# Scores of two neighbourhood heads issued in turn to the two row halves, and scores two heads ahead of the transposes

## The reference

```python
h = rmsnorm_2(x, norm_mix[i])
proj = h @ w_in[i]
na_q, na_k, na_v, q_lat, kv_lat, k_rope, gate_a, gate_b = jnp.split(proj, IN_CUTS, axis=-1)
y_a = neighbourhood_attention(na_q.reshape(B, S, 8, 64), na_k..., na_v..., na_rpb[i]) @ w_na_o[i]
y_b = latent_attention(q_lat, kv_lat, k_rope, ...) @ w_mla_o[i]      # 8 heads, 64 + 32 dims for scores, 64 for values
merged = jax.nn.sigmoid(gate_a) * y_a + jax.nn.sigmoid(gate_b) * y_b
x = x + merged @ w_out[i]
x = x + expert_choice_moe(...)                                       # 16 experts, 384 MB of weights in the two layers
x = x + ple_gate * (p[i] @ ple_w[i])
```

## Time and profile before

| | us |
|---|---|
| median of 3 runs | 1995.76 (1995.65 to 1997.39) |
| the profiled execution | 1993.96 |
| its span in the profile | 1991.8 |
| PE busy | 1591.3 (80%) |
| DVE, ACT, POOL busy | 609.5, 503.2, 188.5 |

### The profile page before, as it was taken

The page is one execution under the profiler, slowest core; times in us unless marked ns, Lnnn a source line. Parts: engine busy times, 40 slices in busy tenths (PEclk is TensorE's granted clock), DMA queues, the critical chain, the costliest instruction groups (busy, mean ns, idle before and its releaser), DMA issues.

```text
span 1991.8 us, 29539 instructions
## 1 busy us (share of the span) xinstructions
PE 1591.3 (80%) x12524; PEld 1158.8 (58%) x12524; DVE 609.5 (31%) x915; ACT 503.2 (25%) x914; POOL 188.5 (9%) x214
## 2 busy tenths in 40 slices
PE   7999999999998998576665666998997566666566
PEld 6999899998897875232222224996774232222225
DVE  3557433676644342000000003554350000000005
ACT  3534233456443432000000003443330000000003
POOL 0042000110321100000000002310100000000002
PEclk9999999999999999887888988998998888888888
DMA  8464748333554319999999997643259999999994
GB/s 286 155 216 156 262 154 264 95 101 114 181 152 151 106 67 425 428 424 423 428 425 425 427 427 291 207 144 135 75 204 427 424 424 427 425 425 427 425 426 140
DMA packets 167949, 563.64 MB, mean 283 GB/s; under 512 B 10591, under 2 KB 122107, under 8 KB 134952
## 3 DMA queue, kind: packets, MB, share of 16 engines
q1 hardware_dynamic: 159952, 552.05, 71.3%
q10 hardware_dynamic: 7896, 10.13, 1.5%
HBM read 561.08 MB, written 5.23 MB: 284 GB/s over the span
## 4 chain that ended last, share of the span: by engine, by line
PE 50%; DMA 38%; DVE 4%; issue 3%; ACT 2%; POOL 1%; ACTq 0%; DVEq 0%; SPq 0%; POOLq 0%
DMA ring<-in_moe_w 36%; PE bank L920 25%; PE bank L1152 6%; PE bank L879 4%; PE bank L1517 3%; PE bank L1210 2%; DMA big<-in_moe_w 2%; PE bank L1050 2%; PE bank L1538 1%; PE bank L1219 1%; PE bank L1082 1%; PE bank L992 1%; DVE ring_r L1985 1%; ACT big L1643 1%; PE bank L1405 1%
## 5 line engine op out<-in xcount | busy, mean ns | idle before, releaser
L1517 PE MATMUL bank<-ring,big 128*32 128x256 f32 x3840 | 284.3, 446 | 198.8 <-DMA ring<-in_moe_w 197.5
L920 PE MATMUL bank<-big_r,ring_r 128*128 128x256 f32 x2736 | 347.8, 288 | 0.0
L1517 PEld LDWEIGHTS bank<-ring,big 128*32 128x32 f32 x3840 | 148.7, 124 | 339.7 <-issue 300.5
L920 PEld LDWEIGHTS bank<-big_r,ring_r 128*128 128x128 f32 x2736 | 339.5, 196 | 1.6 <-issue 0.9
L1985 DVE TENSOR_TENSOR ring_r<-ring,ring_r 128x2048 fp32r<-128x2048 f32 (+2 forms) x105 | 243.3, 2322 | 150.8 <-ACT ring_r L1596 149.6
L1643 ACT ACTIVATE big<-bank 128x512 f32<-128x512 f32 (+2 forms) x186 | 88.0, 490 | 574.5 <-PE bank L879 353.5
L1538 PE MATMUL bank<-ring,big 128*32 128x512 f32 x1024 | 143.9, 653 | 83.0 <-DMA ring<-in_moe_w 65.9
L1596 ACT ACTIVATE ring_r<-ring 128x2048 fp32r<-128x2048 f32 (+2 forms) x109 | 204.2, 1881 | 13.0 <-issue 5.4
L879 PE MATMUL bank<-big 128*128 128x128 f32 (+2 forms) x630 | 106.6, 297 | 66.5 <-ACT big L1643 24.1
L2368 DVE SCALAR_TENSOR_TENSOR big<-big,bank 128x256 f32<-128x256 f32 x32 | 13.5, 421 | 476.4 <-ACT big L1887 476.4
L1152 PE MATMUL bank<-ring_r,big_r 128*128 128x512 f32 x576 | 137.0, 397 | 2.5 <-DVE big_r L1992 2.1
(11 more groups left out here) (198 smaller groups left out, 1422.9 us busy)
## 6 DMA issues: line engine op xcount, KB each, us to landing
ring<-in_moe_w SPq DMA_DIRECT2D x120, 2048.0 KB, 23.7
ring<-in_moe_w SPq DMA_DIRECT2D x128, 1024.0 KB, 25.1
ring<-in_w_in SPq DMA_DIRECT2D x28, 1024.0 KB, 5.4
ring<-in_od_w_in SPq DMA_DIRECT2D x22, 1024.0 KB, 6.7
ring<-in_ev_w_in SPq DMA_DIRECT2D x20, 1024.0 KB, 6.4
big<-in_moe_w SPq DMA_DIRECT2D x8, 2048.0 KB, 20.0
ring<-in_ev_w_out SPq DMA_DIRECT2D x8, 1024.0 KB, 4.9
ring<-in_od_cmp_w SPq DMA_DIRECT2D x8, 1024.0 KB, 8.6
```

Of the source, the lines that this page charges most:

```text
L920: ins = unit[0].mark(mm(dst, lhsT, rhs, start=start and n == 0, stop=stop and n == len(terms) - 1))
L1517: ins = mm(banks[5 + up][32 * j:32 * j + 32, 0:256], xg[:, k, q, :], wv[:, r, 256 * j:256 * (j + 1)], start=k == 0, stop=k == KC - 1)
```

## The change

`paired` now issues the scores of heads 0 and 1 ahead of the first fill, and the scores of head h + 2 directly behind the transposes of head h. This moves the same steps on all four engines. `pT` moves ahead of V14, V15. On PE a new function, `pair_scores`, issues the scores of two neighbourhood heads together: their matmuls alternate between the lower and the upper 64 rows, and go to banks 3 and 4. It stands at the even head's place; at the odd head's PE does nothing. Its wait is that DVE has taken the maximum of the pair before (and so has read both banks). The latent heads keep `scores`. The order on PE becomes:

```diff
@@ paired
-    out = [("S", 0)] + take()
+    out = [("S", 0), ("S", 1)] + take()
     for h in range(heads):
-        if h + 1 < heads:
-            out += [("S", h + 1)]
-        out += [("T", h)] + take()
+        out += [("T", h)] + ([("S", h + 2)] if h + 2 < heads else []) + take()
         if h % 2:
             out += [("V", h - 1), ("V", h)]
@@ LAYER
-         + [(e[0], e[1] + NAH) if e[0] != "proj" else e for e in _ML]
-         + [("pT", 0)] + proj("yb", 0, 1, 2, 3) + [("out", 2)])
+         + [(e[0], e[1] + NAH) if e[0] != "proj" else e for e in _ML[:-2]]
+         + [("pT", 0)] + [(e[0], e[1] + NAH) for e in _ML[-2:]] + proj("yb", 0, 1, 2, 3) + [("out", 2)])
@@ tensor engine
+            def pair_scores(l, h, i):
+
+                if h == 0:
+                    pe.wait_ge(exp_done, 2 * i)
+                    for nm in ("nak", "nav"):
+                        for c in range(2):
+                            wait_evicted(pe, l, nm, c)
+                else:
+                    pe.wait_ge(negmax, i)
+                for t in range(TT):
+                    for n in range(2):
+                        r = slice(NAD * n, NAD * (n + 1))
+                        ins = mm(banks[3 + n][:, t * T:(t + 1) * T], naq[r, h // 2, t * P:(t + 1) * P], nak[r, h // 2, :],
+                                 start=True, stop=True)
+                        if t == TT - 1:
+                            ins.then_inc(sc_done, 1)
@@ the loop over LAYER
+                    elif what == "S" and kind == "na":
+                        if h % 2 == 0:
+                            pair_scores(l, h, att_at(l, h))
                     elif what == "S":
                         scores(l, h, att_at(l, h), kind)
```

More of the change, by code:

```diff
@@ L1031, in scores @@
                     wait_evicted(pe, None, kind + "_mk", h // 2), wait_evicted(pe, None, kind + "_xq", h // 2)
[L1032 to L1035, removed]
                 if kind == "ml" and h == 0:
@@ L1044, in scores @@
                         q, k = q[:, h, t * P:(t + 1) * P], k[:, h, :]
-                    elif kind == "na":
-                        r = slice(NAD * (h % 2), NAD * (h % 2) + NAD)
-                        q, k = naq[r, h // 2, t * P:(t + 1) * P], nak[r, h // 2, :]
                     else:
```

## The result

| | before | after |
|---|---|---|
| median, us | 1996.58 (1995.65 to 1998.68, 4 runs) | 1964.47 (1963.62 to 1967.51, 4 runs) |
| span of the profiled execution | 1991.8 | 1961.5 |
| PE, DVE, ACT busy, us | 1591.3, 609.5, 503.2 | 1583.3, 609.5, 502.5 |

The ratio is 0.984, with a 95% interval of 0.9823 to 0.9858: 32 us faster. The forecast was 1964.8. Five more runs of the changed kernel on another occasion gave 1964.51, ratio 0.9839 (0.9826 to 0.9853).

What follows compares the result with a forecast made beforehand. The prediction took PE's order to bound the stretch ahead of the experts, which go at their weights' pace. Its terms, 8.5 + 13.25 + 8.8 + 0.5 = 31.0 us, off 1995.76 gave 1964.8 us, own range 1959 to 1970, with rivals to 1975.

Steps and rivals of the forecast that it cites:

- PE's order bounds the stretch: In the neighbourhood heads PE's order sets the time; gains ahead of the experts' weight stream count in full.
- Part 1: Neighbourhood scores: two heads on separate row halves overlap, a pair taking one head's 1.06 us; gain 8.5 us.
- The rival without overlap: Neighbourhood scores: row halves don't overlap, a pair costs 1.94 us, 7.0 us dearer, 1971.8; chance 0.06.
- lower bound: Neighbourhood scores: gain of only 1.4 us without any overlap, also expected had both heads gone to one bank.
- Part 2: End of the neighbourhood heads, T6 to LN: earlier scores cover head 7's relay, wait and half clock go; gain 13.25 us.
- The reckoning of the relay: Head 7's bias to normalisation, counted from S0: bias at 45.3, end at 49.2, T7 at 50.5; slack about 1.5 us.
- Part 3: End of the latent heads, T14 to yb 0, with pT moved: falls to 3.9 us; gain 8.8 us, moving pT alone nothing.
- The remaining 0.5 us: In yb 0 to 3: half clock reaching into yb 0 goes, 0.5 us for both layers.
- Part 4: What moves costs nothing: latent scores only change places, the pair's new wait and later splits stay covered.
- The sum: All gains together, 8.5 + 13.25 + 8.8 + 0.5 = 31.0 us, giving 1964.8 us against the median.
- a gain that the experts give back: Rival in the experts: their stream starts earlier but ends at the same time, 1995.8; chance 0.02.
- the slower rival: Neighbourhood heads: the pair's shared wait breaks the relay's lead, nine waits a layer, 54 lost against 31 gained, 2018; chance 0.03.

Runs made afterwards that it cites:

- same_half: Changed kernel, but both heads of a pair read the lower 64 rows: 1971.94 us against 1964.51 for the changed kernel beside it.
- pT_behind: Changed kernel with pT back behind V14V15: 1964.83 us, ratio 0.9843 to the kernel before.
- heads_in_turn: Changed kernel with the two-head scores' loops swapped, both matmuls of the even head before both of the odd: 1963.88 us, ratio 0.9846 to the kernel before.
- na_only: The change in the neighbourhood heads alone, latent heads and pT in the order of before: 1973.6 us against 1995.78 for the kernel before, ratio 0.9892.
- late_wait_and_split: Changed kernel, yb 0 waiting for heads 14, 15 only at its last quarter, gb 2's split moved behind head 8's scores: 1957.17 us, ratio 0.9803 to before.

## Why the prediction was right

- **PE's order bounds the stretch, and its gain reaches the end.** Right. From S0 to LN in layer 1 it now takes 57.86 us (1280.22 to 1338.08) where it took 68.78. The first expert loads went out 14.3 and 30.1 us earlier, and the span is 30.3 us shorter: the experts gave nothing back and added nothing.
- **Part 1, 8.5 us.** Right in size and right in its cause (the row halves, by same_half). The idea with which I went into the runs was refuted: I took the overlap to need alternation, since the only pattern in the trace alternated. The rival without overlap (a pair at 1.94 us, 7.0 us dearer) is what same_half measured: 1.92 and 7.4. All runs wrote the two heads to two banks, so what one bank for both would cost, which the prediction put at the 1.4 us of its lower bound, no run shows.
- **Part 2, 13.25 us.** S0 to LN shrank by 10.92 and 10.57 us. Less 4.24 for the pairs that leaves 6.7 and 6.3, 13.0 in all. The reckoning of the relay can be read off the trace of after. Counted from S0 at 1280.22, head 7's bias was due at 45.3 us and starts at 45.4, its normalisation was due to end at 49.2 and ends at 49.3, and T7, due at 50.5, starts at 50.6 inside the entry of T6 and T7. The slack is 1.3 us; the prediction's own numbers gave 1.3 too, and it wrote "about 1.5".

```profile
1325.60 0.68 DVE L2276 SCALAR_TENSOR_TENSOR big<-bank,big 128x512 f32<-128x512 f32 x1
...
1328.48 1.04 POOL L2465 TENSOR_TENSOR big<-big 128x512 f32<-128x512 f32 x1 [5.60 <-DVE big L2099]
```

  LN was reckoned to have 0.6 us to spare behind `latent`; in the trace `latent` ends at 1336.77 and LN starts at 1338.08, 1.3 to spare. The second reduction of `latent` takes 0.56 us there and took 1.27 before, when it ran beside POOL's normalisation; that the one is the cause of the other is not shown.
- **Part 3, 8.8 us.** T14 to yb 0 is 4.04 us in both layers where 3.9 was forecast: gain 4.52 and 3.99, 8.5. Moving pT alone was worth nothing, as said (pT_behind).
- **The remaining 0.5 us** in yb 0 to 3: 14.05 us where it was 14.28. Right.
- **Part 4, no cost.** Right: the pair's new wait never stopped PE. It does at 0.72 us more a head.
- **The sum** was 31.0 us; layer by layer the traces give 14.9 and 16.05 us from S0 to the first expert load, 31.0. The parts make 30.5 of it; the other 0.5 lies between LN and T14, in a stretch to which the prediction gave only a spread of some 2 us a layer. The spans differ by 30.3 as the time ahead of layer 0's attention and in the experts varies by a microsecond between executions, and the medians by 32.1, within their interval of 28 to 35. That the median came within 0.4 us of the forecast is luck: the gain was 1.1 us more than the sum, and the median of before, with its fourth run, 0.8 us above the one that the forecast started from.

What carried the forecast was that the unknown parts had a twin in the trace: the pair had the earlier trace rows, the tails could be put together from durations at full clock. One slip stands in the chances: 0.02 for a gain that the experts give back and 0.03 for the slower rival became 0.01 for no change and 0.04 for slower.

## What to carry to other kernels

Heads of 64 dimensions lie two to a tile: issue the scores of both next to each other on TensorE, into two banks, and the second is free; in this kernel the order of the matmuls within didn't matter. A wait of TensorE can cost more than its idle time, since the granted clock falls behind it: 36 needless transposes in one wait of 4.00 us bought 2.5 us. When an order is made dense, reckon the relay of the other engines per head against TensorE's time per head, and look for prefetch work (here splits) that stands ahead of something TensorE waits for, while the same engine idles elsewhere.

## What the runs showed of the hardware that I had not expected

- Matmuls on different row halves run side by side even when both of one head are issued ahead of both of the other: eight records in 1.07 us in either order, 1.92 with all in one half. The Trainium skill, "TensorE: Matmul & The Clock Gate", section "Part 2: What happens when you issue a matmul", says that matmuls stay in program order and only weight loads are pulled ahead. The records of heads_in_turn don't agree with it across row halves: two of them start within the first 0.2 us, 13 ns apart. Started in program order, the first record of the odd head would have come behind all four of the even head, and the pair, overlapped only where the heads meet, would have taken some 1.7 us (an estimate: 1.92 less one record of 0.22). This takes the program to have reached the chip in the order in which it is written, which the trace does not show by itself.
- From the first scores of a layer to yb 0, half clock (0.5 of full speed) came with every wait of 3.05 us or more, in some cases before the wait had ended, and with none of 1.28 us or less. The waits of 2.70 us ahead of QT 2 had it in both layers of before, of after and of eight further runs, and in layer 0 of na_only, but not in its layer 1 (the wait of 2.70 that ends at 1364.51 us):

```profile
1361.00:1373.00 12.00, 9.30 (x73) 8.69 (x72) 7.77 (x6) 8.41 (x14) 1.04 (x1) 1.00 0.10 41
```

  So the same wait can come with half clock or without it. In late_wait_and_split, with that wait at 0.91 us, the granted clock stayed at 1.00 over the 150 us of the window above.
